# Seven half-size products for two pairs of tiles in a cross-attention output projection

## What is computed

```python
def _memory_xattn(h, mem, w_q, w_k, w_v, w_o):
    ...
    o = jnp.einsum('bhqk,bkhd->bqhd', p, v).reshape(b, s, D_MODEL)
    return o @ w_o
...
        xa = _memory_xattn(h, m, w_cq[l], w_ck[l], w_cv[l], w_co[l])
        h = _layer_norm(DEEPNORM_ALPHA * h + xa, ln2_g[l], ln2_b[l])
        ff = _hier_moe(h, w_router_g[l], b_router_g[l], w_router_e[l], b_router_e[l],
                       w_e_gate[l], w_e_up[l], w_e_down[l])
```

## Time and profile before

| | us |
|---|---|
| three runs | 1066.18, 1067.60, 1068.52 (median 1067.6) |
| the profiled execution | 1068.76 |
| its span, first to last instruction | 1067.0 |
| PE busy in the span | 944.7 (89%) |
| DVE busy | 469.6 (44%) |
| POOL busy | 299.5 (28%) |
| ACT busy | 224.7 (21%) |
| mean granted PE clock | 0.94 |

### The profile page before, as it was taken

The page is one execution under the profiler, slowest core; times in us unless marked ns, Lnnn a source line. Parts: engine busy times, 40 slices in busy tenths (PEclk is TensorE's granted clock), DMA queues, the critical chain, the costliest instruction groups (busy, mean ns, idle before and its releaser), DMA issues.

```text
span 1067.0 us, 10055 instructions
## 1 busy us (share of the span) xinstructions
PE 944.7 (89%) x3384; PEld 495.0 (46%) x3384; DVE 469.6 (44%) x738; ACT 224.7 (21%) x541; POOL 299.5 (28%) x344
## 2 busy tenths in 40 slices
PE   4899999799999899999999999958988999999900
PEld 3456466344544444445567445446434444444300
DVE  5589999964622233726234132262311111111156
ACT  2412123234492121001014211030101111111111
POOL 5712032334453232200014221102161211211137
PEclk9899999899999999999999999965998999999955
DMA  9410301303002001320050430072797999999562
GB/s 326 170 40 0 119 1 54 103 1 80 1 21 98 1 0 35 123 79 1 0 196 2 167 137 31 40 293 101 323 409 285 415 420 421 393 410 378 196 239 118
DMA packets 46231, 166.13 MB, mean 156 GB/s; under 512 B 8514, under 2 KB 13890, under 8 KB 33892
## 3 DMA queue, kind: packets, MB, share of 16 engines
q1 hardware_dynamic: 39460, 152.88, 37.3%
q0 software_dynamic: 6720, 12.60, 3.2%
HBM read 157.92 MB, written 18.03 MB: 165 GB/s over the span
## 4 chain that ended last, share of the span: by engine, by line
PE 57%; DVE 3%; POOL 3%; issue 2%; DMA 2%; POOLq 0%; ACT 0%; SPq 0%; DVEq 0%
PE ps L1710 12%; PE ps L2116 8%; PE ps L2145 7%; PE ps L1984 7%; PE ps L2119 5%; PE ps L1957 5%; PE ps L1891 2%; PE ps L1816 2%; PE ps L2093 2%; PE ps L1788 2%; PE ps L2048 2%; POOL hres L685 1%; PE ps L1719 1%; PE ps L2013 1%; DMA hT<-h_rows,gidx 1%
## 5 line engine op out<-in xcount | busy, mean ns | idle before, releaser
L1710 PE MATMUL ps<-ring,hT 128*128 128x512 f32 (+1 forms) x384 | 145.6, 540 | 0.9 <-issue 0.9
L1218 DVE SCALAR_TENSOR_TENSOR cat<-early,cpar,cat 128x798 f32<-128x798 f32 x120 | 131.2, 1094 | 3.8
L1710 PEld LDWEIGHTS ps<-ring,hT 128*128 128x128 f32 x384 | 72.6, 190 | 71.1 <-issue 68.7
L787 POOL TENSOR_SCALAR hT<-hT,rinv 128x512 f32<-128x512 f32 (+1 forms) x48 | 67.8, 1424 | 96.6 <-DVE rinv L1315 96.6
L1710 PE MATMUL ps<-hT,ring 128*128 128x256 f32 (+1 forms) x256 | 87.9, 507 | 0.9 <-issue 0.7
L853 POOL DMA_INDIRECT pair_rows<-hT,sidx x22 | 22.0, 1001 | 182.5 <-DVE hT L1637 181.7
L1710 PEld LDWEIGHTS ps<-hT,ring 128*128 128x128 f32 x256 | 50.9, 200 | 36.3 <-issue 31.3
L1627 DVE COPY memx<-ps 128x256 f32<-128x256 f32 x22 | 9.3, 424 | 131.2 <-PE ps L2128 131.2
L674 POOL TENSOR_SCALAR lnt<-mv 128x1 f32<-128x1 f32 x28 | 12.9, 459 | 176.9 <-DVE mv L702 176.3
L2145 PE MATMUL ps<-ring,memx 128*64 128x512 f32 (+1 forms) x144 | 60.1, 612 | 0.7 <-DVE memx L1627 0.7
L794 POOL TENSOR_SCALAR memx<-memx,rinv 128x256 f32<-128x256 f32 x24 | 22.1, 924 | 130.2 <-DVE rinv L1273 130.2
(11 more groups left out here) (293 smaller groups left out, 1613.8 us busy)
## 6 DMA issues: line engine op xcount, KB each, us to landing
ring<-w_down SPq DMA_DIRECT2D x16, 1024.0 KB, 17.1
early<-w_gate SPq DMA_DIRECT2D x12, 1024.0 KB, 10.3
early<-w_up SPq DMA_DIRECT2D x12, 1024.0 KB, 14.8
ring<-w_gate SPq DMA_DIRECT2D x10, 1024.0 KB, 13.1
ring<-w_up SPq DMA_DIRECT2D x10, 1024.0 KB, 16.6
scr<-w_down SPq DMA_DIRECT2D x8, 1024.0 KB, 15.7
cat<-w_down SPq DMA_DIRECT2D x8, 1024.0 KB, 15.4
scr<-w_gate SPq DMA_DIRECT2D x5, 1024.0 KB, 10.4
```

Source lines behind the costliest of these rows:

```text
L787: g.tensor_scalar(sprob[u % 4][:, 0:width], sprob[u % 4][:, 0:width], rinv[:, u % 4:u % 4 + 1], None, ALU.mult).then_inc(prob_ready, 1)
L1218: ins = v.scalar_tensor_tensor(out=acc[:, c, :], in0=src, scalar=cpar[:, c, k:k + 1], in1=acc[:, c, :], op0=ALU.mult, op1=ALU.add)
L1710: last = t.matmul(out_of(bank), lhs(k), rhs(k), start=(k == 0), stop=(k == KC - 1))
```

## The change

Tiles 0 and 1, and tiles 2 and 3, are computed as a pair. The rows of a pair and the 1024 inner channels are each split into two halves, and so are the channels and columns of the weight: A11 and A12 are the odd tile's two halves of channels, A21 and A22 the even tile's; B00, B01, B10, B11 are the quarters of `w_co`. Seven products of four matmuls each (128 rows, 512 channels, 512 columns) replace eight, after Winograd's form of Strassen's scheme. Around them DVE makes

- four sums of quarters of the weight: T3 = B11 - B01 and T2 = T3 + B00, in halves of 1024 columns behind units 10, 12, 14 and 16 of the softmax loop; T4 = B10 - T2 and T1 = B01 - B00 (2048 columns) behind the cross attention;
- for each pair four sums of rows, S1 to S4 (512 columns each);
- for each pair eleven sums of 512 columns that put the products together with the residual in `hres`, in place of four residuals.

ACT evicts P1 of each pair. Tiles 4 and 5 stay as they were. The transposes of normed rows and the router products move back against the products: those of tile 0 stand inside the second pair, those of tile 1 behind it, and five router products stand behind or between the products of tiles 4 and 5. The work areas of the sums lie where the weights of expert 1 and the down weights of expert 0 are loaded to, so these three loads move behind the last product of the second pair.

```diff
@@ plan_banks
-    for i in range(NT + 1):
+    for a in range(CO_PAIRS):
+        for term in TERMS:
+            take("mm", ("co7", a, term))
+    for i in range(2 * CO_PAIRS, NT):
...
@@ SP
             load_gu(0, 0)
-            load_d(0, 0)
-            load_gu(1, 1)
             load_gu(2, 2)
             for i in range(NT):
+                if i == 2:
+                    full(sp, ("co7", CO_PAIRS - 1, TERMS[-1]))
+                    load_d(0, 0)
+                    load_gu(1, 1)
                 sp.wait_ge(ln_done, LN_2[i] + 1)
                 sp.dma_start(h2_dram[i * P:(i + 1) * P, :], hres[:, i, :]).then_inc(h2_stored, 16)
@@ ACT
-            for k, n in enumerate(LN_2):
-                if k >= 1:
-                    rows_T(2, k - 1)
-                act_hat(act, n)
-            rows_T(2, NT - 1)
+            for a2 in range(CO_PAIRS):
+                bank = full(act, ("co7", a2, "P1"))
+                a.activation(coU[a2], bank, ACT.Copy).then_inc(free(("co7", a2, "P1")), 1)
+            act_hat(act, LN_2[0])
+            act_hat(act, LN_2[1])
+            rows_T(2, 0)
+            rows_T(2, 1)
+            act_hat(act, LN_2[2])
+            act_hat(act, LN_2[3])
+            rows_T(2, 2)
+            act_hat(act, LN_2[4])
+            for i in range(3, NT):
+                rows_T(2, i)
@@ DVE
+            def co_weights(n):
+                h = slice(1024 * (n % 2), 1024 * (n % 2) + 1024)
+                slab_wait(dve, "co0")
+                slab_wait(dve, "co1")
+                if n < 2:
+                    v.tensor_tensor(coT["T3"][:, h], coB[1][1][:, h], coB[0][1][:, h], ALU.subtract).then_inc(co_combined, 1)
+                else:
+                    dve.wait_ge(co_combined, 2)
+                    v.tensor_tensor(coT["T2"][:, h], coT["T3"][:, h], coB[0][0][:, h], ALU.add).then_inc(co_combined, 1)
...
+                    if u in CO_WEIGHTS_AT:
+                        co_weights(CO_WEIGHTS_AT[u])
...
+            def term_sum(a, term):
+                e, l = 2 * a, 2 * a + 1
+                f = free(("co7", a, term))
+                if term == "P2":
+                    was_read(dve, ("co7", a, "P1"))
+                    link(with_residual(l, 0, coU[a]))
+                    add_term(a, term, l, 0).then_inc(f, 1)
+                elif term == "P6":
+                    v.tensor_tensor(coU[a], full(dve, ("co7", a, term)), coU[a], ALU.add).then_inc(f, 1)
+                    was_read(dve, ("co7", a, term))
+                    link(with_residual(l, 1, coU[a]))
+                elif term == "P7":
+                    v.tensor_tensor(coV[a], full(dve, ("co7", a, term)), coU[a], ALU.add).then_inc(f, 1)
+                    was_read(dve, ("co7", a, term))
+                    with_residual(e, 0, coV[a])
+                    link(with_residual(e, 1, coV[a]))
+                elif term == "P4":
+                    add_term(a, term, e, 0).then_inc(f, 1)
+                elif term == "P5":
+                    add_term(a, term, e, 1)
+                    add_term(a, term, l, 1).then_inc(f, 1)
+                    was_read(dve, ("co7", a, term))
+                else:
+                    add_term(a, term, l, 1).then_inc(f, 1)
+                    was_read(dve, ("co7", a, term))
+
+            for j in range(2):
+                was_read(dve, ("xO", CROSS[-1][0], j))
+            row_sums(0, 0)
+            row_sums(0, 1)
+            v.tensor_tensor(coT["T4"], coB[1][0], coT["T2"], ALU.subtract).then_inc(co_combined, 1)
+            v.tensor_tensor(coT["T1"], coB[0][1], coB[0][0], ALU.subtract).then_inc(co_combined, 1)
+            for term in TERMS[1:6]:
+                term_sum(0, term)
+            dve_stats(dve, LN_2[0], link)
+            term_sum(0, "P3")
+            row_sums(1, 0)
+            dve_stats(dve, LN_2[1], link)
+            row_sums(1, 1)
+            term_sum(1, "P2")
+            dve_bias(dve, LN_2[0], link)
+            term_sum(1, "P6")
+            term_sum(1, "P7")
+            dve_bias(dve, LN_2[1], link)
+            term_sum(1, "P4")
+            term_sum(1, "P5")
+            dve_stats(dve, LN_2[2], link)
+            term_sum(1, "P3")
+            dve_stats(dve, LN_2[3], link)
+            for k in range(2 * CO_PAIRS, NT):
                 for j in range(2):
                     residual(("co", k, j), k, j).then_inc(free(("co", k, j)), 1)
+                    if k == 4:
+                        dve_bias(dve, LN_2[2 + j], link)
                     was_read(dve, ("co", k, j))
-                dve_stats(dve, n, link)
+                dve_stats(dve, LN_2[k], link)
+                if k == 4:
+                    dve_bias(dve, LN_2[4], link)
             dve_bias(dve, LN_2[-1], link)
@@ PE
+            for a in range(CO_PAIRS):
+                (A11, A12), (A21, A22) = co_rows(a)
+                co_term(a, "P1", A11, coB[0][0])
+                co_term(a, "P2", A12, coB[1][0])
+                pe.wait_ge(co_combined, 6 + 6 * a)
+                co_term(a, "P6", coS["S2"], coT["T2"])
+                pe.wait_ge(co_combined, 7 + 6 * a)
+                co_term(a, "P7", coS["S3"], coT["T3"])
+                if a == 0:
+                    pe.wait_ge(co_combined, 9)
+                else:
+                    h2_T(0)
+                co_term(a, "P4", A22, coT["T4"])
+                if a == 0:
+                    pe.wait_ge(co_combined, 10)
+                co_term(a, "P5", coS["S1"], coT["T1"])
+                pe.wait_ge(co_combined, 8 + 6 * a)
+                co_term(a, "P3", coS["S4"], coB[1][1])
+            h2_T(1)
+            for i in range(2 * CO_PAIRS, NT):
+                for j in range(2):
+                    last = product(("co", i, j), lambda k: k, lambda k: hTv[:, k, i * P:(i + 1) * P],
+                                   lambda k: wo[j][:, k, :])
+                    done(("co", i, j), last)
+                    if j == 0:
+                        route(i - 4)
+                h2_T(i - 2)
+            route(2)
+            h2_T(NT - 2)
+            route(3)
+            h2_T(NT - 1)
+            route(4)
             done("route", route(NT - 1))
```

More of the change, by code:

```diff
@@ L104 @@
 CQ_CHUNKS = KC // 2
+CO_PAIRS = 2
+CO_WEIGHTS_AT = {10: 0, 12: 1, 14: 2, 16: 3}
 TH = T // 2
@@ L221, in plan_banks @@
             take("pv", ("xO", n, j))
-    for i in range(NT + 1):
+    for a in range(CO_PAIRS):
+        for term in TERMS:
+            take("mm", ("co7", a, term))
+    for i in range(2 * CO_PAIRS, NT):
         for j in range(2):
-            if i < NT:
-                take("mm", ("co", i, j))
+            take("mm", ("co", i, j))
+    for i in range(NT):
         for j in range(2):
-            if i >= 1:
-                take("tr", ("hT", 2, i - 1, j))
+            take("tr", ("hT", 2, i, j))
     take("pv", "route")
@@ L306, in cv_out, with co_rows @@
             return vm[:, MT // 2 * h + i, 512 * j:512 * (j + 1)]
+        co_at = [(slab_names.index(f"co{j}") % 3) for j in range(2)]
+        coB = [[ring[:, co_at[j], 2048 * k:2048 * (k + 1)] for j in range(2)] for k in range(2)]
+        co3 = 3 - sum(co_at)
+        coT = {"T3": ring[:, co3, 0:2048], "T2": ring[:, co3, 2048:4096], "T4": early[:, 4096:6144], "T1": early[:, 6144:8192]}
+        coS = {f"S{n + 1}": scr[:, 4096 + 512 * n:4608 + 512 * n].rearrange("p (k t) -> p k t", k=4) for n in range(4)}
+        coU = [memx[:, 1024 * a:1024 * a + 512] for a in range(CO_PAIRS)]
+        coV = [memx[:, 1024 * a + 512:1024 * a + 1024] for a in range(CO_PAIRS)]
+        def co_rows(a):
+            return [[hTv[:, 4 * k:4 * k + 4, i * P:(i + 1) * P] for k in range(2)] for i in (2 * a + 1, 2 * a)]
         cq_at = [(slab_names.index(f"cq{j}") % 3) for j in range(2)]
@@ L439, in encoder @@
         u_ready = sem("u_ready")
-        combined, cv_combined = sem("combined"), sem("cv_combined")
+        combined, cv_combined, co_combined = sem("combined"), sem("cv_combined"), sem("co_combined")
         qkv_raw, rot_ready = sem("qkv_raw"), sem("rot_ready")
@@ new lines, in half_row, with with_residual, add_term @@
+            def half_row(i, j):
+                return hres[:, i, 512 * j:512 * (j + 1)]
+            def with_residual(i, j, term_sum):
+                return v.scalar_tensor_tensor(out=half_row(i, j), in0=half_row(i, j), scalar=ALPHA, in1=term_sum,
+                                              op0=ALU.mult, op1=ALU.add)
+            def add_term(a, term, i, j):
+                return v.tensor_tensor(half_row(i, j), half_row(i, j), full(dve, ("co7", a, term)), ALU.add)
+            def term_sum(a, term):
[23 more added lines that the diff above has]
+                    was_read(dve, ("co7", a, term))
@@ L2018, in _, with co_term, h2_T @@
             logits = claim("route")
[L2019 to L2030, removed]
+            def co_term(a, term, rows, w):
+                bank, wk = claim(("co7", a, term)), w.rearrange("p (k c) -> p k c", k=4)
+                for k in range(4):
```

(8 more changed lines are left out.)

12 lines of the change are left out of this document (9 added, 3 removed).

## The result

The changed kernel takes **1058.88 us** (median of 5 runs, 1056.23 to 1059.42), the kernel before beside it 1067.6 (5 runs, 1065.09 to 1068.52): a ratio of 0.9923 [0.9906, 0.994]. Two later sets of runs gave 0.9933 [0.9911, 0.9955] and 0.9929 [0.9913, 0.9945]. The forecast was 1061.1, its range 1056.5 to 1066.0. The profiled execution took 1058.15 us, its span 1056.4.

What follows compares the result with a forecast made beforehand. PE's matmuls were taken to bound the projection, with later stages sliding with its end. Terms -6.9 + 1.0 - 0.7 - 0.8 + 0.8 = -6.6, called -6.5, gave 1061.1 us against median 1067.6; range 1056.5 to 1066.

Steps and rivals of the forecast that it cites:

- The matmuls, -6.9: Projection: seven products a pair instead of eight save 8 matmuls of 0.863 us on PE's gapless path, -6.9 us.
- The softmax, +1.0: Softmax loop: DVE weight sums at units 12 and 16 delay PE's turning by 0.49 us each, +1.0 us together.
- Ports: New two-input DVE sums meet POOL in SBUF: 0.1 to 0.2 us for each softmax rescale, nothing added to the sum.
- -5.2: Forecast total in us if DVE and POOL fully exclude each other, sums at units 12 and 16 starting up to 0.7 later.
- Row sums, other weight sums, assembly, loads: 0: Projection: DVE's sums are covered by PE's products, and the moved expert loads have 65 us of cover; cost nothing.
- The end, -0.7 and -0.8: End of projection: PE's wait for norm 5 shrinks from 1.86 to about 1.2 us; router product 4 covers ACT's copy.
- The clock, +0.8: End of projection: clock falls between last transposes and router product 4, 1.92 - 0.87 saved, 1.9 lost, +0.8 us.
- The ends, -2.9 and +1.9: Bounds in us at the projection's end: clock full throughout, -2.9, or at half from the last transposes on, +1.9.
- rival 1: Clock stays full to the end of the router products: -10.3 us, about 1057.3; chance 0.13.
- Rival 2: DVE becomes the bound in pair 1 of the projection, half the gain goes: 1063 to 1065.5 us; chance 0.18.
- Rival 3: Something behind the router does not slide, a late transfer eats the gain: 1067.6 us, no change; chance 0.06.
- Rival 4: Softmax pauses at the turning of units 10, 12, 14 and 16 halve the clock: about 1075 us, slower; chance 0.08.

Runs made afterwards that it cites:

- experiment 2: The changed kernel with one of the seven products of each pair made twice, giving back 8 matmuls; median 1066.3 us, ratio to before 0.9988.
- experiment 4: The changed kernel with two expert loads moved on behind the last product of tile 5; median 1061.53 us, beside 1061.93 for the changed kernel.
- experiment 1: The changed kernel with the softmax loop's four weight sums behind units 9, 11, 15 and 19; median 1056.87 us, ratio to before 0.990.
- experiment 3: The kernel before with only the end of the projection in the changed kernel's order; median 1063.25 us, ratio to before 0.9964.

## Why the prediction was right, step by step

**The matmuls, -6.9.** Right in size and cause: 24.1 us a pair, and 6.88 us for 8 matmuls when they are put back (experiment 2).

**The softmax, +1.0.** Right in mechanism and place: two waits of PE, at the turning of units 12 and 16, none for the sums of units 10 and 14. It measured +1.36, because a sum that starts just behind POOL's rescale takes 0.19 us more. The forecast named such an effect under *Ports*, 0.1 to 0.2 each, and left it out of the sum. What is lost hangs on which starts first: the sum of 568.50, 0.15 us behind a rescale of 0.92 us, loses 0.19 us, and the rescale of 575.19, 0.01 us behind a sum of 1.22 us, loses 1.07. The Trainium skill (SBUF — State Buffer, Who interferes with whom) has the later of such a pair wait for all of the earlier. The trace comes near that where the sum is first, and not where the rescale is. The sums at units 12 and 16 stand behind their rescales, so the -5.2 that the prediction worked out by that rule didn't come.

**Row sums, other weight sums, assembly, loads: 0.** Right. No PE wait in the two pairs, none at the transposes of tiles 0 to 4, and loads that can go out 38 us later still (experiment 4). In the projection one bias on DVE, started 0.47 us behind a POOL multiply, took 2.96 us instead of 1.23, and one multiply 2.70 instead of 2.34, with no PE wait behind either.

**The end, -0.7 and -0.8.** Right: 0.82 and 0.78. The norm's 6.12 us are 6.13 here (residual at 683.86, transposes at 689.99).

**The clock, +0.8.** This is the step that failed: "I put the fall between transposes and router product 4". It came some 1.5 us later, inside router product 4, so the term was -0.83 in this execution: the transposes gained, the router products lost nothing. In the other two traces of the changed kernel the transposes ran at full clock too, and the term was +0.15 and 0.00 by the length of products 4 and 5. The ends, -2.9 and +1.9, hold every trace with this order of work: products 4 and 5 took from 3.66 us, rival 1's case (experiment 1), to 6.88 (experiment 3, where the clock fell in the transposes). With the measured terms the sum reads -6.9 + 1.36 - 0.82 - 0.78 - 0.83 = -8.0, within 0.1 us of what the stages show. In the three traces of the changed kernel products 4 and 5 took 5.47, 6.45 and 6.30 us. The Trainium skill (TensorE: Matmul & The Clock Gate, Part 1) says of the clock's rise that the number of matmuls at the low clock differs between runs of the same kernel; these three traces show the like for a fall. The clock's term is no fixed one, and the three medians of the changed kernel lie 8.7, 5.3 and 7.3 us below those of before, on both sides of the forecast's 6.5: how near a set of runs comes to it is in part luck.

**The rivals.** Rival 1 (full clock) was seen without filling in one trace, that of experiment 1, and in none of the three of the changed kernel. Rival 2 (DVE) falls with experiment 2. Rival 3 falls with the stage table: the first expert product starts 9.9 us earlier (731.44 against 741.34), 8.0 of them by the change, the last product 9.9 too, and routing and experts keep their lengths. Rival 4 falls because the pauses are 0.49 us, and the clock is 1.00 over the whole attention stage.

Of the profiled execution's 10.6 us, 2.5 are not the change: 1.86 ahead of the cross attention and 0.67 at the very end, where the code is the same.

## What to carry to other kernels

Where PE runs without a gap, a product saved is its whole duration, and sums on an idle engine that replace it are free, as long as each stands ahead of a gap of that engine; put them by the timeline of the waiting engine, not at equal distances. Cut a profile at the same events in both kernels, since 2 us of scatter in unchanged stages look like an effect. A short wait of PE can cost more behind it than in it: with eight passes whose result nobody reads in a wait of 1.04 us, the work behind it took 1.7 us less in the mean of the traces (the medians side by side differ by 1.0), and filling the waits of the routing as well gave the largest gain of this study, though not in every execution.

## What the runs showed that was not expected

- The granted clock falls from 2.4 to 1.2 GHz at different points of the same program: behind the same wait of 1.04 us, two router products took 3.66, 5.43, 5.47, 6.30, 6.45 or 6.49 us, the first of these in a kernel that differs only 100 us earlier. What decides the point was not found. This one line makes up nearly all the difference between the projection's lengths, 92.9 to 95.7 us in the kernels that make 28 matmuls a pair.
- Half clock is worth real time in a stage that looks bound by chains of small DVE work: 3.2 us of 35 in the routing in one of the two filled traces, none in the other, and in both 1.3 to 2.7 in the first expert block behind it (7.09 us against 8.4 to 9.8).
- A DVE sum with both inputs in SBUF and a POOL rescale of 256 columns run beside each other where the rescale starts first: 1.41 us instead of 1.22 for the sum. Where the sum starts first, the rescale takes 1.99 us instead of 0.92.
